# A two-layer streaming trunk: the query GEMM reads the unscaled residual, and the RMS factor of each token goes into the gates' exponential

## What is computed

```
h = h + cat(mixers) @ w_out
xn = rms(h) * g                      # per token: h / sqrt(mean(h^2) + eps), per channel: g
q = xn @ wq                          # 8 heads x 2 halves x 128
s = q . keys                         # 128 scores for each token, head and half
top 16 of each half, top 16 of their 256 sums -> expert numbers, values fv
gate = softmax(fv)                   # per token and head
out = sum(gate * gelu(xn . u[e]) * v[e])
```

## Time and profile before

| | |
|---|---|
| time, median of 3 runs | 1869.92 us (1866.32 to 1876.38) |
| the profiled execution | 1865.88 us, its span 1864.0 us |
| TensorE busy | 1783.0 us, 96% |
| VectorE busy | 1452.3 us, 78% |
| ScalarE, GpSimd busy | 837.5 us, 875.0 us |
| mean granted clock of TensorE | 0.973 of full |

### The profile page before, as it was taken

How to read it: one execution, slowest core, us unless ns; L and a number is a source line. 1 busy time by engine, 2 the same in 40 slices (tenths; PEclk the granted TensorE clock), 3 DMA queues, 4 the chain that set the end, 5 groups by cost and what they waited for, 6 DMA issues and landing times.

```text
span 1864.0 us, 39016 instructions
## 1 busy us (share of the span) xinstructions
PE 1783.0 (96%) x14384; PEld 1735.8 (93%) x14384; DVE 1452.3 (78%) x3027; ACT 837.5 (45%) x1771; POOL 875.0 (47%) x635
## 2 busy tenths in 40 slices
PE   9978899999999899999999788999999999999999
PEld 8966899999999899999989768999999999999998
DVE  2686558895499889999946755688644998999997
ACT  6523441211476545555546225412114776555543
POOL 4895560234143447676437964602341333554540
PEclk9979899999999999999999878999999999999999
DMA  5400345899899899999944002568998997999995
GB/s 197 136 2 2 104 157 192 304 402 391 340 349 339 299 345 415 420 419 412 392 141 155 2 2 91 173 205 315 375 409 304 328 339 279 381 388 391 387 385 188
DMA packets 138648, 505.84 MB, mean 271 GB/s; under 512 B 15392, under 2 KB 15520, under 8 KB 138272
## 3 DMA queue, kind: packets, MB, share of 16 engines
q1 hardware_dynamic: 87840, 319.68, 46.2%
q0 software_dynamic: 50688, 184.57, 26.0%
HBM read 503.14 MB, written 1.05 MB: 270 GB/s over the span
## 4 chain that ended last, share of the span: by engine, by line
PE 69%; DVE 20%; DMA 5%; issue 4%; ACT 2%; SPq 0%; ACTq 0%; POOL 0%; DVEq 0%; POOLq 0%
PE ps L1100 69%; DMA w<-v_c 5%; DVE arena L2164 3%; DVE onehots_i L2096 2%; DVE rows_w L1942 2%; DVE w_lo L2148 1%; DVE x_hi L2140 1%; DVE arena L2117 1%; DVE rows_x L1942 1%; ACT w_hi L789 1%; DVE x L1662 1%; DVE x_lo L1655 1%; DVE arena L1677 1%; DVE arena L1707 1%; DVE onehots_j L1650 0%
## 5 line engine op out<-in xcount | busy, mean ns | idle before, releaser
L1100 PE MATMUL ps<-x_hi,w_hi 128*128 128x352 f32 (+2 forms) x2544 | 721.8, 342 | 20.6 <-DVE x_lo L1655 10.9
L1100 PE MATMUL ps<-x_hi,w_lo 128*128 128x176 f32 (+2 forms) x2544 | 646.8, 254 | 0.0
L1100 PE MATMUL ps<-x,w 128*128 128x176 f32 x4096 | 627.8, 313 | 0.0
L1100 PEld LDWEIGHTS ps<-x,w 128*128 128x128 f32 x4096 | 612.5, 190 | 0.6 <-issue 0.2
L1100 PEld LDWEIGHTS ps<-x_hi,w_hi 128*128 128x128 f32 x2544 | 480.0, 189 | 35.3 <-DVE x_hi L2140 10.1
L1100 PEld LDWEIGHTS ps<-x_hi,w_lo 128*128 128x128 f32 x2544 | 485.7, 191 | 0.0
L789 ACT CAST w_hi<-w 128x1024 fp32r<-128x1024 f32 x318 | 334.2, 1051 | 318.2 <-DMA w<-v_c 234.0
L717 POOL DMA_INDIRECT arena<-v_c,sel x176 | 311.3, 1769 | 226.4 <-DVE arena L2164 199.6
L685 POOL TENSOR_TENSOR w_lo<-w,w_hi 128x1024 fp32r<-128x1024 f32 x90 | 222.4, 2485 | 211.7 <-ACT w_hi L789 211.6
L2148 DVE TENSOR_TENSOR w_lo<-w,w_hi 128x1024 fp32r<-128x1024 f32 x228 | 278.0, 1219 | 32.2 <-ACT w_hi L789 31.6
L717 POOL DMA_INDIRECT rows_w<-ur_c,sel x116 | 120.7, 1040 | 232.5 <-DVE sel L1942 222.7
(11 more groups left out here) (196 smaller groups left out, 1739.5 us busy)
## 6 DMA issues: line engine op xcount, KB each, us to landing
w<-u_c SPq DMA_DIRECT2D x256, 512.0 KB, 5.7
w<-v_c SPq DMA_DIRECT2D x256, 512.0 KB, 6.5
w<-w_c SPq DMA_DIRECT2D x84, 512.0 KB, 3.5
arena<-v_c,sel POOLq DMA_INDIRECT x176, 8.2
arena<-keys_c SPq DMA_DIRECT2D x2, 1024.0 KB, 8.3
arena<-mix_c SPq DMA_DIRECT2D x2, 964.0 KB, 8.8
rows_w<-ur_c,sel POOLq DMA_INDIRECT x116, 7.9
h<-h SPq DMA_DIRECT2D x2, 544.0 KB, 5.0
```

The lines of the kernel that those rows point to most:

```text
L1100: return nc.tensor.matmul(out_, lhsT, rhs, start=start, stop=stop, skip_group_check=True)
```

## The change

- `raw_high` and `raw_low` split `h * g` (without the factor) into `raw_hi` and `raw_lo`, chunk by chunk in the loop of the output GEMM: ScalarE scales and casts chunk `m - 1` ahead of squaring it, VectorE multiplies and subtracts behind its add of chunk `m`. They lie in the arena, where earlier activations are dead by then.
- The query GEMM reads these two. Its first two tiles wait for the adds that free their banks. `square_sums` stands behind query tile 0; the 14 matmuls on zeros are gone.
- ScalarE's root stands behind its evacuation of query tile 0; its 8 casts of `xn` are gone. VectorE's norm makes `xn` alone, without the 8 low parts.
- Behind query tile 2 TensorE turns the factors to one per partition (`turn_scales`: 6 small matmuls in layer 0, 2 in layer 1); ScalarE copies them behind its tile 4, and the gates' exponential takes them as its scale.
- `xs_rep` is a copy of `xn` in place of hi + lo; it is turned behind query tiles 7, 11 and, in layer 0, 15, and copied back behind tiles 8, 12 and 15.
- `restore` is gone. The keys' load waits for the first add of the output GEMM.

```diff
@@ sync
-                sp.wait_ge(s_xn, (2 * l + 2) * DC)
+                sp.wait_ge(s_ed, l * NOUT + 1)
                 sp.dma_start(keys.rearrange("p m n -> p (m n)"), keys_c[l]).then_inc(s_keys, 16)
@@ scalar
+            def raw_high(l, t0, c):
+
+                act.wait_ge(s_ed, l * NOUT + c + 1)
+                nc.scalar.activation(raw_hi[:, c, t0:T], h[:, c, t0:T], ACT.Identity,
+                                     scale=vcol(l, "norm2", c)).then_inc(s_xh, 1)
...
                 for m in range(NOUT):
                     high(l, NZ + m + AHEAD)
                     if m:
+                        raw_high(l, L.t0, m - 1)
                         square(l, 1, m - 1)
+                raw_high(l, L.t0, NOUT - 1)
                 square(l, 1, NOUT - 1)
-                norm_scale(l, 1)
-                x_high(l, 2, xn, L.t0)
...
+                def keep_turned(x):
+
+                    act.wait_ge(s_xr, X0[l] + x + 1)
+                    nc.scalar.copy(xs_rep[x][:, 0:HALF], ps[:, X_BANKS[x][0], :])
+                    nc.scalar.copy(xs_rep[x][:, HALF:D], ps[:, X_BANKS[x][1], :]).then_inc(s_xrc, 1)
+
                 for m in range(NQ):
+                    evacuate(l, NZ + NOUT + m, pq[:, m, L.t0:T], L.nt)
                     if m == 0:
-
-                        act.wait_ge(s_xn, (2 * l + 2) * DC)
-                    evacuate(l, NZ + NOUT + m, pq[:, m, L.t0:T], L.nt)
...
+                        norm_scale(l, 1)
+                    if m == 4:
+                        act.wait_ge(s_rt, l + 1)
+                        nc.scalar.copy(scale_t[:, 0:2 * len(L.tiles)], ps[:, 3, 0:2 * len(L.tiles)]).then_inc(s_rk, 1)
+                    if m % 4 == 0 and m // 4 - 2 in range(len(L.groups)):
+                        keep_turned(m // 4 - 2)
...
+                if len(L.groups) == 3:
+                    keep_turned(2)
                 scores(L.scores[6:])
...
-                        ins = nc.scalar.activation(gates_, gates_, ACT.Exp)
+                        ins = nc.scalar.activation(gates_, gates_, ACT.Exp, scale=scale_t[:, 2 * s:2 * s + 1])
@@ tensor
-                square_sums(l, 1)
-                warm(WARM["norm"], 3)
+
+                def turn_scales():
+
+                    pe.wait_ge(s_xn, (2 * l + 1) * DC + 1)
+                    for s, (t0, nt) in enumerate(L.tiles):
+                        for q in range(PACK if L.tiles[s] == PACKED else 1):
+                            r = slice(32 * q, 32 * q + 32) if L.tiles[s] == PACKED else slice(0, nt)
+                            last = mm(ps[r, 3, 2 * s:2 * s + 2], var[:, t0:t0 + r.stop - r.start], ident[:, 0:2], True, True)
+                    last.then_inc(s_rt, 1)
...
-                    project(l, n, L.t0, ready=None if m else x_split(l, 2))
-                    x = m // 4
-                    if m % 4 == 3 and x < len(L.groups):
+                    else:
+                        pe.wait_ge(s_ed, l * NOUT + NOUT - 1 + m)
+                    project(l, n, L.t0, ready=None if m else x_split(l, 2), hi=raw_hi, lo=raw_lo)
+                    if m == 0:
+                        square_sums(l, 1)
+                    if m == 2:
+                        turn_scales()
+                    x = m // 4 - 1
+                    if m % 4 == 3 and x in range(len(L.groups)):
...
-                        pe.wait_ge(s_xf, l + 1)
+                        pe.wait_ge(s_xn, (2 * l + 2) * DC)
@@ vector
-                    if c:
-                        x_low(l, 2 * k, xn, xl, t0, c - 1)
-                x_low(l, 2 * k, xn, xl, t0, DC - 1)
+                    if c and not k:
+                        x_low(l, 0, xn, xl, t0, c - 1)
+                if not k:
+                    x_low(l, 0, xn, xl, t0, DC - 1)
+
+            def raw_low(l, t0, c):
+
+                dve.wait_ge(s_xh, (3 * l + 2) * DC + c + 1)
+                v.scalar_tensor_tensor(raw_lo[:, c, t0:T], h[:, c, t0:T], vcol(l, "norm2", c),
+                                       raw_hi[:, c, t0:T].bitcast(F32), ALU.mult, ALU.subtract).then_inc(s_xl, 1)
...
                                     ALU.add).then_inc(s_ed, 1)
+                    if m:
+                        dve.wait_ge(s_ed, l * NOUT + m)
+                        raw_low(l, L.t0, m - 1)
                     if 2 <= m <= SQ_DVE:
                         add_square(l, m - 1)
                 dve.wait_ge(s_ed, (l + 1) * NOUT)
+                raw_low(l, L.t0, NOUT - 1)
                 norm(l, 1, L.t0)
-                dve.wait_ge(s_xl, (3 * l + 3) * DC)
+                dve.wait_ge(s_xn, (2 * l + 2) * DC)
...
-                    v.tensor_tensor(xs_rep[x].rearrange("p (c q t) -> p c q t", c=DC, q=rep),
-                                    bc(xh[:, :, w].bitcast(F32), 2, rep), bc(xl[:, :, w].bitcast(F32), 2, rep),
-                                    ALU.add).then_inc(s_xd, 1)
+                    v.tensor_copy(xs_rep[x].rearrange("p (c q t) -> p c q t", c=DC, q=rep),
+                                  bc(xn[:, :, w], 2, rep)).then_inc(s_xd, 1)
...
-                restore()
                 run(first_level(0, 3))
```

More of the change, by code:

```diff
@@ L87 @@
 ARENA = 31744
+RAW_AT = NMIX + 4 * P + DC * T
 SCORE_LAG = 4
@@ L309, in trunk @@
         zero_t = sb("zeros", P + 2)
-        arena_t = sb("arena", ARENA)
+        scale_t = sb("token_scales", 2 * NT)
+        with nc.sbuf_tensor("arena", [P, ARENA], F32) as arena_t:
+            pass
+        sb("below_raw", RAW_AT)
+        raw_lo_t = sb("raw_low", DC * T, F32R)
+        sb("between_raw", NZ * (T + 1) - DC * T)
+        raw_hi_t = sb("raw_high", DC * T, F32R)
+        sb("above_raw", ARENA - RAW_AT - NZ * (T + 1) - DC * T)
         ps = ctx.enter_context(nc.psum_tensor("ps", [P, 8, 512], F32))
@@ L315, in trunk @@
         xn, xh, xl = tok(xn_t), tok(xh_t), tok(xl_t)
+        raw_hi, raw_lo = tok(raw_hi_t), tok(raw_lo_t)
         vecs = vec_t[:, :].rearrange("p (l n) -> p l n", l=DEPTH)
@@ L368, in trunk @@
         mixed_end = A.at
+        assert mixed_end == RAW_AT + NZ * (T + 1) + DC * T
         def two(n=T):
@@ L555, in trunk @@
         s_xd = sem("gathered_tokens_x_replicated")
-        s_xf = sem("x_restored")
+        s_rt = sem("token_scales_turned")
+        s_rk = sem("token_scales_kept")
         s_xr = sem("gathered_tokens_x_in_psum")
@@ L1027, in exps @@
                     asked()
+                    act.wait_ge(s_rk, l + 1)
                     for s in tiles:
                         gates_ = chosen[:, s, 0, 0:P // PACK if L.tiles[s] == PACKED else P]
-                        ins = nc.scalar.activation(gates_, gates_, ACT.Exp)
+                        ins = nc.scalar.activation(gates_, gates_, ACT.Exp, scale=scale_t[:, 2 * s:2 * s + 1])
                     ins.then_inc(s_ad, 1)
@@ L1135, in tile, with project @@
                 last.then_inc(s_use, 1)
[L1137 to L1140, removed]
+            def project(l, n, t0=0, ready=None, order=range(DC), hi=xh, lo=xl):
+                o = ps[:, 1 + n % 2, 0:T - t0]
+                tile(l, n, lambda c: o, lambda c: hi[:, c, t0:T], lambda c: lo[:, c, t0:T], 0, ready, order)
             def attention(l):
@@ L1923, in _ @@
                 g_idx = g_at.bitcast(U32)
[L1925 to L1931, removed]
                 dots = [0]
```

## The result

| | before | changed |
|---|---|---|
| first session, median | 1868.29 us (4 runs) | 1851.45 us (1849.54 to 1852.21, 4 runs) |
| ratio, 95% interval | | 0.9882 (0.9846 to 0.9917) |
| second session, median | 1868.96 us (30 runs) | 1855.08 us (1848.35 to 1864.05, 7 runs) |
| ratio, 95% interval | | 0.9929 (0.9900 to 0.9957) |
| the profiled execution | 1865.88 us | 1850.99 us |

The change is faster in both sessions, by about 1%. One of the 30 runs took 2097.96 us at a granted clock of 0.779 and is not part of the ratio. The first ratio is 22 us, the second 13; the profiled executions differ by 14.9, and the two medians of the first session by 16.8. The forecast of 14.2 us lies inside the second interval and short of the first.

A forecast was written before the change was run, and what follows sets the result against it. TensorE, busy 96% of the span, was taken as the bound. Layer 0: 9.0 - 1.4 - 0.46 - 0.3 + 0.4 = 7.2; layer 1: 8.9 - 1.4 - 0.46 = 7.0; together 14.2 us, so 1855 us, range 1847 to 1864.

The forecast's parts named there:

- The mechanism and the gap: Ahead of the query GEMM: with raw_hi and raw_lo, tile 0 ends 9.0 us earlier in layer 0, 8.9 in layer 1.
- Sums: Behind query tile 0: three square sums now lie on TensorE's path, 0.46 us each, 1.4 per layer.
- The wait covered at the last scores of layer 0: The third turned group lies between tile 15 and its scores, covering TensorE's 0.47 us wait for ScalarE's copy: 0.4 gained.
- Rival 2: The wait only moves: TensorE waits for the factor behind query tile 2, the gain shrinks or goes, 1870 us; chance 0.06.
- rival 3: Slower: without zeros the clock falls in the query GEMM, 3.02 us more per tile, up to 1904 us; chance 0.03.
- Rival 4: More: TensorE's unexplained 5.11 us wait may vanish in the changed program, giving 1850 us; chance 0.08.
- VectorE. Seven multiplies more at 0.41 to 0.49 end near 228.1: Layer 0's norm: after the first multiply at 225.1, VectorE's seven others take 0.41 to 0.49 us each, ending near 228.1.
- The replications: VectorE, behind the norm's multiplies: three replications, as copies, take the same 7.9 us as before, to 236.0.
- no change: Query GEMM: the turned groups of replicated activations are the same number, only later, 1.7 us each, so they cost nothing.
- TensorE waits only for the add, which stays first: End of the output GEMM: VectorE's add precedes raw_low and a square's add, at most 0.5 us each, hidden by matmuls.
- rival 1: Part is given back, in the query GEMM or the full VectorE stage: about half, 7 us, for 1863; chance 0.12.
- The median lies 4.0 above that execution and the runs spread over 10 us: Step from the profiled execution's 1851.7 us to a predicted median of 1855.7, rounded down to 1855 for the spread.

The follow-up runs named there:

- fillers: Matmuls on zeros in two of TensorE's waits ahead of the output GEMM, added to the changed kernel with one sum and reciprocals in PSUM: 0.9902, 1849.07 us.

## Why the prediction was right and wrong

**The mechanism and the gap: right.** Tile 0 ends 2.99 us after the start of the last add, against 12.01 before: 9.0 off, as forecast. Sums 1.37 (1.4), turned factors 0.71 (0.76), no wait behind tile 2, no wait for `raw_lo` or `w_lo` in either query stage. The wait covered at the last scores of layer 0 was priced at 0.4; turning late is worth 0.7 there, by the run that turns early with quick products. The later stages are nearly unchanged: from the first hidden tile to the first output expert it takes 348.9 to 349.0 us in layer 1, and in layer 0 364.7 to 364.9 in the three profiles without the change and 364.9 to 365.8 in the ten with it. So about 0.5 us may be given back there; no run asked why. Rival 2 didn't occur, and rival 3 only where a run put a gap or a wait back. Rival 4 didn't either, the 5.11 us are still there in the changed kernel:

```profile
632.56 5.11 issue
```

**The step of the mechanism that failed: "VectorE. Seven multiplies more at 0.41 to 0.49 end near 228.1".** They ended at 235.6. I took the duration from a row during which GpSimd was idle (it started at 229.35) and moved it beside GpSimd. The replications went wrong the other way: as two-input adds the first, which started ahead of GpSimd, took 1.23 us and the two behind it 3.42 each, so the 7.9 that I carried over to the copies had held-up time in it. I asked for the replications whether the copies could hold GpSimd up, and did not ask which way the products would be held. The Trainium skill, page "SBUF — State Buffer", in its practical consequences, says that a VectorE instruction with two SBUF inputs contends with a GpSimd one that reads SBUF, and that the order of issue decides who blocks. The traces agree: 11.13 us against 3.36 with one operand in PSUM, and a single add 2.64 against 0.43. The stage's size came out right all the same because turns stand four tiles later, which the prediction priced at "no change" and which is worth 7.9 us in each layer. That is luck: the forecast had the right sum over a wrong account of what protects it.

**"TensorE waits only for the add, which stays first": wrong in layer 1.** The add stood behind a square's add held up by GpSimd. From the first to the last add the stage is 1.0 us longer, and that 1.0 is gone in the run that moved the square's add. It is a small part of rival 1.

**Sizes.** Layer 0's stage gave 8.1 us for the forecast 7.2. Two terms make most of the difference: 0.7 for the 0.4 at the last scores, and 0.5 for query tiles that take 2.99 us where they took 3.03, which I had put at nothing. Layer 1 gave 7.9, less 1.0 for the late add: 6.9 against 7.0. Together 15.0, ratio 0.992, or 14.5 if the hidden stage of layer 0 gives 0.5 back. The sum of 14.2 was right to within 1 us.

**The step that failed for the time: "The median lies 4.0 above that execution and the runs spread over 10 us".** It treated the 4.0 us as an offset and let the range end 8 us below the forecast. It is scatter, and wider: the first ratio's 22 us and the second's 13 come from the same two kernels, and the query stages of a profile from either session hold about 15. Thirteen profiles put the largest part of it ahead of the last add of layer 0, between 215.5 and 228.1 us, and there it goes with the time that the clock is low: 30.7 us low gives 215.5 and 215.7, 58.0 gives 223.8, 64.9 gives 228.0 and 228.1. In between it is less exact: 44.4 gives 220.2 and 220.3, and 47.8 gives 218.8, 219.5 and, with fillers, 221.5. The output experts add some 4 us in either layer. For the 6 us between the two profiles of before the 216 matmuls above show it in the rows, without an edit; that the clock makes the rest is argued from the thirteen, and only the part at the first output tile was changed by an edit. That the 7 us of the first ratio above these 15 are scatter is argued too, with four runs a side.

**Open.** Why query tiles are 0.03 to 0.04 us shorter: the place of the operands explains at most half in layer 0. What decides when the clock is low in the mixing, what sets the output experts' scatter, and why layer 0's hidden stage is longer, was not tried.

## What to carry to other kernels

When work is moved, take its duration from a row with the same neighbours: an instruction that took 0.42 us in a gap took 1.39 on average beside GpSimd. If a gain hangs on an idle margin, undo each "harmless" reordering by itself: here two of them, the late turns and the early load, carried all and most of the gain. And where executions scatter by more than the effect, size it by a stage of the trace that repeats (0.02 us here), not by medians of a few runs, and look beside that stage for what was given back.

## What the hardware showed that I had not expected

VectorE's product with two SBUF operands waited for a whole GpSimd subtraction: eight in 11.13 us against 3.36 with one of the two in PSUM, while GpSimd's 2.4 us stayed as it was. The replication as a copy took 0.69 us for each group free of GpSimd and 2.89 when it met it; as a two-input add it took 1.23 where it started ahead of GpSimd and 3.42 where it started behind. A wait of 5.0 us of TensorE cost 7.2 in all (7.9 less the 0.7 that early turns cost without any wait): the clock was at its lower level, 1.2 GHz, for 6.8 us, the last 4.1 of them behind the wait. And with the same code in the mixing the last add of layer 0 came up to 12.6 us earlier or later, along with 30.7 to 64.9 us of low clock.
